# An adaLN hybrid backbone on one core: sums of squares taken inside the projections, residual additions followed block by block, and modulation rounds moved

## Chip, cores and metric

One core of a Trainium2 chip runs the whole program as one launch. The metric is the device time of an execution in microseconds (us). The kernel was timed three times before the change. One further execution was profiled; every row shown here comes from it.

## What is computed

Two layers run over 256 context tokens and 256 latent tokens, with D = 1024, all in float32. Only the latent tokens are returned.

```
x <- x + gate * RMSNorm_post(F(RMSNorm_pre(x) * (1 + scale) + shift))
m = SiLU(c) @ W_mod[layer] + b_mod[layer]      # (shift, scale, gate) for 2 sub-layers: 6 x 1024
layer 0: F = chunked gated linear attention, then dense SwiGLU (1024 -> 2816 -> 1024)
layer 1: F = RWKV-7 time mixing (latent output only), then top-2-of-8 SwiGLU experts (latent only)
rmsnorm(x, g) = x * rsqrt(mean(x*x) + 1e-6) * g
```

Context tokens have a modulation row of their own, from the same weights `W_mod`. In layer 1 the scan of the latent tokens starts from the final state of the scan of the context tokens.

## The kernel before

**Layout.** Activations lie transposed in SBUF: 128 partitions of features, 8 blocks of features (`KT = 8`), 512 tokens (`TOK`, columns 0 to 255 context, 256 to 511 latent). `X` is the residual stream. Everything is scheduled by hand: each engine has its own straight program, and waits on semaphores order them. A wait holds back everything behind it on its engine.

**A norm** (`norm_stats(n, width)`, once for ScalarE and once for TensorE) goes block by block. ScalarE squares block k into one of two buffers of `sq` and raises `sq_ready`. TensorE multiplies it by a matrix of ones and accumulates in PSUM bank 7, raising `sq_used`. After eight blocks ScalarE takes the root into `std`. VectorE then takes the reciprocal (L1367). For a norm ahead of a sub-layer VectorE multiplies `X` by it (`normalise`, L1374), and ScalarE applies the modulation (`modulate`, L1082, `h_ready` for each block). For a norm behind a sub-layer, `post` multiplies the output (L1381) and adds it to `X` with the gate (L1384), one `post_done` for each block, waiting for it before the next block. The norms are numbered: 0 ahead of attention, 1 behind its output projection `gla_o`, 2 ahead of the dense SwiGLU, 3 behind it, 4 and 5 ahead of the time mixing (context, latent), 6 behind its output projection `rw_o`, 7 ahead of the experts. All eight squares of a norm follow the end of what feeds it: for norms 2, 4, 5 and 7 the last residual addition, for 1, 3 and 6 the last copy out of PSUM.

**Modulation** comes in six rounds of 2048 columns (0 to 2 for layer 0, 3 to 5 for layer 1). A round reads 8 MB of `mod_w` as eight chunks of 1 MB. `mod_step(r, k, bank)` (L564) is TensorE's work on a chunk. VectorE copies the bank out (`mod_copy`, L1394), TensorE turns it (`mod_select`, L573, 8 matmuls), VectorE adds the bias (`add_bias`, L1400), then `pre_gains` and `post_gains` combine it with the norm's gains. Round 3 stands ahead of norm 2, round 4 between norm 2 and the dense SwiGLU, and round 5 between norm 3 and norm 4. Round 3 holds shift and scale of the time mixing (norms 4 and 5), round 4 its gate and the shift of the experts, round 5 scale and gate of the experts.

**Weights** stream through a ring of six 1 MB slots, all issued by SyncE in the order of the list `chunks`; the load of chunk n waits until chunk n-6 has been used. The ring is scratch memory during the RWKV scans, so the first chunk of `rw_k1` waits for the end of the context scan. GpSimd loads the small RWKV matrices (2.75 MB, `rw_small`) once for each segment, the second time after the context scan.

**Layer 1** runs `segment(0)` (norm 4, mixes, projections), the context scan, `segment(1)` (norm 5 and the same for latent tokens), the latent scan, the output projection `rw_o` and norms 6 and 7. In a segment VectorE prepares up to six mixes in two buffers `XJ` (`mix`, L1577). TensorE runs `hidden` on the first mix (L771), its second matrices (L782), then `hidden` on the second mix, and so on. The expert stage (L1011 to L1043) loops over eight experts, with rings of its own for its weights.

**The dense SwiGLU** has eleven pairs of up projections (L738, a block is 8 matmuls of 128x512) and a down projection (L748) that accumulates all eight output blocks over eleven chunks in the eight banks. Only when the last chunk is done does ScalarE copy out the eight banks (L1181, `O2`).

## Time and profile before

| | us |
|---|---|
| median of three runs | 2811.93 |
| lowest, highest | 2807.17, 2813.3 |
| the profiled execution | 2807.7 |
| its span, first to last instruction | 2805.9 |
| TensorE busy in it | 2576.8 |

The profiled execution takes 1.8 us more than its span. Times in rows count from the start of the span. A row of the timeline gives the start, the duration, the engine, the line of the kernel, the operation, what it writes and reads, how many instructions were merged, and in brackets the idle time ahead of it with what ended it. One float32 matmul of the kernel's code appears as two MATMUL records, so that the 64 matmuls of a projection of eight blocks are x128.

### The profile page before, as it was taken

To read this page: it belongs to the slowest core of one execution; us is meant where nothing else is said; L and a number is where in the kernel's file an instruction comes from. 1 tells how busy PE (TensorE), PEld (TensorE's weight loads), DVE (VectorE), ACT (ScalarE), POOL (GpSimd) and SP (SyncE) were. 2 spreads that over 40 slices of the span, in tenths; PEclk is the share of its full clock that TensorE was granted. 3 is DMA by queue.
4 is the path that set the end of the run, shared out by engine and by line. 5 is a ranking of instruction groups with operands and counts; after the bars stand their busy time and mean duration, and the time that the engine had idled before them with its cause. 6 is when DMAs were issued, how large, how long until landed. Compare 5 with 4: busy or idle time off the path is not lost.

```text
span 2805.9 us, 60500 instructions
## 1 busy us (share of the span) xinstructions
PE 2576.8 (92%) x27787; PEld 1788.2 (64%) x27788; DVE 664.7 (24%) x1098; ACT 468.3 (17%) x781; POOL 45.9 (2%) x146
## 2 busy tenths in 40 slices
PE   6998878999999878869888779999999999999998
PEld 2562732444444357868787578686969696959593
DVE  1033433100000176764876420000000010000001
ACT  3232012100000143443333120000000000000000
POOL 0000001200000000000000000000000000000000
PEclk9998979999999979989999789999999999999999
DMA  6215104622222320042002248888889897979794
GB/s 244 76 60 224 61 15 188 196 75 75 75 75 75 113 96 2 4 131 90 2 4 72 83 145 321 300 324 301 318 304 327 294 338 283 348 274 349 272 345 145
DMA packets 179201, 492.90 MB, mean 176 GB/s; under 512 B 9410, under 2 KB 73236, under 8 KB 172804
## 3 DMA queue, kind: packets, MB, share of 16 engines
q1 hardware_dynamic: 177156, 482.73, 48.3%
q0 software_dynamic: 1792, 6.19, 0.7%
q8 instruction: 232, 3.80, 0.5%
q14 instruction: 21, 0.17, 0.0%
HBM read 487.84 MB, written 1.05 MB: 174 GB/s over the span
## 4 chain that ended last, share of the span: by engine, by line
PE 53%; DVE 5%; ACT 1%; issue 1%; DMA 0%; POOL 0%; DVEq 0%; ACTq 0%; POOLq 0%
PE banks L1026 25%; PE banks L1043 14%; PE banks L809 6%; PE banks L606 3%; PE banks L1000 1%; PE banks L942 1%; PE banks L1011 1%; DVE ring_arena L1678 1%; PE banks L771 1%; DVE ring_arena L1683 1%; DVE rstd L1789 0%; DMA ring_arena<-in_rw_a 0%; PE banks L782 0%; DVE ring_arena L1690 0%; PE banks L543 0%
## 5 line engine op out<-in xcount | busy, mean ns | idle before, releaser
L1026 PEld LDWEIGHTS banks<-ring_arena 128*64 128x64 f32 x14336 | 687.1, 137 | 19.2 <-issue 18.4
L1026 PE MATMUL banks<-ring_arena 128*64 128x112 f32 x14336 | 694.2, 259 | 0.0
L1043 PE MATMUL banks<-ring_arena 128*112 128x512 f32 x896 | 385.8, 592 | 0.0
L606 PE MATMUL banks<-ring_arena 128*128 128x256 f32 (+1 forms) x1024 | 313.0, 467 | 24.4 <-ACT ring_arena L1082 12.7
L738 PE MATMUL banks<-ring_arena 128*128 128x512 f32 x704 | 305.3, 597 | 0.0
L1043 PEld LDWEIGHTS banks<-ring_arena 128*112 128x112 f32 x896 | 158.0, 177 | 221.9 <-issue 221.9
L606 PEld LDWEIGHTS banks<-ring_arena 128*128 128x128 f32 x1024 | 196.5, 193 | 140.3 <-issue 96.4
L1872 DVE TENSOR_TENSOR ring_arena<-ring_arena,banks 128x448 f32<-128x448 f32 x32 | 19.9, 621 | 1033.3 <-PE banks L1026 1033.3
L738 PEld LDWEIGHTS banks<-ring_arena 128*128 128x128 f32 x704 | 134.8, 192 | 169.8 <-issue 169.8
L809 PE MATMUL banks<-ring_arena 64*64 64x128 f32 (+1 forms) x6144 | 205.2, 260 | 31.2 <-DVE ring_arena L1683 13.1
L809 PEld LDWEIGHTS banks<-ring_arena 64*64 64x64 f32 x6144 | 192.8, 138 | 38.4 <-issue 22.7
L748 PE MATMUL banks<-ring_arena 128*128 128x512 f32 x352 | 151.3, 592 | 0.9 <-DVE ring_arena L1528 0.9
L748 PEld LDWEIGHTS banks<-ring_arena 128*128 128x128 f32 x352 | 66.8, 190 | 85.4 <-issue 83.7
L1367 DVE RECIPROCAL rstd<-std 128x512 f32<-128x512 f32 (+1 forms) x12 | 33.8, 2819 | 310.3 <-ACT std L1075 301.1
L1336 ACT ACTIVATE ring_arena<-banks 128x448 f32<-128x448 f32 x32 | 17.4, 544 | 512.7 <-PE banks L1026 512.7
L1242 ACT COPY ring_arena<-banks 128x1024 f32<-128x1024 f32 (+1 forms) x80 | 72.2, 928 | 111.4 <-DVE ring_arena L1678 98.3
L1108 ACT ACTIVATE ring_arena<-banks 128x256 f32<-128x256 f32 (+2 forms) x94 | 40.5, 439 | 284.7 <-PE banks L606 178.1
L1528 DVE TENSOR_TENSOR ring_arena<-ring_arena,banks 128x512 f32<-128x512 f32 x22 | 15.1, 687 | 290.2 <-PE banks L738 290.2
L564 PE MATMUL banks<-ring_arena 128*32 128x512 f32 x384 | 56.4, 700 | 20.0 <-DMA ring_arena<-in_mod_w 17.6
L543 PE MATMUL banks<-sq_ntmp,ones 128*128 128x256 f32 (+1 forms) x112 | 49.0, 588 | 26.3 <-ACT sq_ntmp L1073 25.5
L1326 ACT COPY ring_arena<-banks 112x512 f32<-112x512 f32 x18 | 9.6, 588 | 372.5 <-PE banks L1043 372.5
L1178 ACT ACTIVATE ring_arena<-banks 128x512 f32<-128x512 f32 x22 | 13.1, 597 | 278.6 <-PE banks L738 278.6
(293 smaller groups left out, 1827.8 us busy)
## 6 DMA issues: line engine op xcount, KB each, us to landing
ring_arena<-in_moe_w_gu SPq DMA_DIRECT2D x256, 896.0 KB, 5.5
ring_arena<-in_moe_w_d SPq DMA_DIRECT2D x112, 1024.0 KB, 7.1
ring_arena<-in_mod_w SPq DMA_DIRECT2D x48, 1024.0 KB, 7.3
ring_arena<-in_ff_w_gu SPq DMA_DIRECT2D x22, 1024.0 KB, 5.1
ring_arena<-in_rw_w_rkv SPq DMA_DIRECT2D x20, 1024.0 KB, 10.9
ring_arena<-in_gla_w_in SPq DMA_DIRECT2D x12, 1024.0 KB, 5.4
ring_arena<-in_ff_w_d SPq DMA_DIRECT2D x11, 1024.0 KB, 4.9
ring_arena<-in_gla_w_out SPq DMA_DIRECT2D x4, 1024.0 KB, 13.8
```

Of the source, the lines that this page charges most:

```text
L543: T.matmul(ps[7][:, 0:width], ones[:, :], sq[:, (k % 2) * TOK:(k % 2) * TOK + width], start=(k == 0), stop=(k == KT - 1)).then_inc(S["sq_u ...
L564: ins = T.matmul(bank[32 * j:32 * j + 32, :], csil[r // 3][:, k, :], w[:, j, :], start=(k == 0), stop=(k == KT - 1))
L606: ins = T.matmul(b[:, 0:width], w[:, k, j * P:j * P + P], src[:, k, :], start=(k == 0), stop=(k == KT - 1))
L738: ins = T.matmul(ps[4 * (p % 2) + 2 * ab + j][:, :], w[:, k, j * P:j * P + P], H2[:, k, :], start=(k == 0), stop=(k == KT - 1))
L748: ins = T.matmul(ps[j][:, :], w[:, k, j * P:j * P + P], HID[:, 2 * i + k, :], start=(i == 0 and k == 0), stop=(i == FT // 2 - 1 and k == 1))
L771: ins = T.matmul(b[0:cols, 0:SEG], w[:, k, :], src[:, k, :], start=(k == 0), stop=(k == KT - 1))
L809: ins = T.matmul(bank[rows[1 - r if cross and p >= HP // 2 else r], p, 0:x.shape[-1]], lhs[rows[r], p, :], x, start=first and p % (HP // 2 ...
L1026: ins = T.matmul(bank[CH * h:CH * h + CH, (c % 4) * CAP:(c % 4) * CAP + CAP], w[:, kk, c * P + CH * h:c * P + CH * h + CH], XG[:, 2 * kp + ...
L1043: ins = T.matmul(ps[6 + h][0:CAP, :], HX[:, 2 * u + k, :], w[:, k, 512 * h:512 * h + 512], start=(u == 0 and k == 0), stop=(u == WD_UNITS ...
L1108: C.activation(dst, src, func, **kw).then_inc(S["pj_out"], 1)
L1242: C.copy(w[d]["ZT"][:, :, half], scan_banks(d, 0)[:, :, half]).then_inc(za_s[d], 1)
L1367: link(Vv.reciprocal(rstd[:, 0:width], std[:, 0:width]))
```

## The change

The sum of squares of norms 1, 3 and 6 is taken inside the projection that feeds it: ScalarE squares each block right after it has copied it out, and TensorE takes the matmul with ones (`stat`) two blocks later, between the matmuls of the projection (for norm 3 in bank 0, within the last chunk of the down projection). The squares of norms 2, 4, 5 and 7 each wait for their own block's residual addition alone. Behind the dense SwiGLU, `post_half(0)` adds the context half to `X` first; the latent half follows within `segment(0)`, between the first and the second mix. Round 3 is wound into norm 2 and round 4 into norm 4 (`between_stats`); round 5 moves to the latent segment, between norm 5 and the first `hidden`. Their `mod_select`s stand in the second pair of up projections and ahead of the key projections. The first up projection waits for `h_ready` block by block. `O2` has another layout, and a third copy of SiLU(c) lies in `masks2`.

```diff
+        mod_rows = [ntmp[:, 512 * (r % 2):512 * (r % 2) + 512] if r < 3 else (at(22016, 512) if r == 3 else ntmp[:, 512:1024]) for r in range(6)]
 
...
         H2 = at(0, KT, TOK)
         HID = at(4096, FT, TOK)
         SIL = at(15360, 4, TOK)
...
         KK, KEY = at(0, SC, HP, CH), at(2048, SC, HP, CH)
         AA = [at(4096 + 2048 * d, SC, HP, CH) for d in range(2)]
@@ -223,7 +223,7 @@
...
         n_pairs = FT // 2
...
-        stream("ff_d", [A["ff_w_d"][0].rearrange("(k p) n -> p k n", p=P)[:, 2 * i:2 * i + 2, :] for i in range(11)], "ffd", 0, 1)
-        stream("mod5", mod_rounds(1, 2), "mod_mm", 40, 1)
+        ffd_views = [A["ff_w_d"][0].rearrange("(k p) n -> p k n", p=P)[:, 2 * i:2 * i + 2, :] for i in range(11)]
+        stream("ff_d", ffd_views[0:10], "ffd", 0, 1)
+        stream("ff_d_last", ffd_views[10:11], "ffo", 0, KT)
+        stream("mod4", mod_rounds(1, 1), "mod_mm", 32, 1)
...
         for sg in range(2):
+            if sg:
+                stream("mod5", mod_rounds(1, 2), "mod_mm", 40, 1)
             for n, name in ((1, "k"), (2, "v"), (0, "r"))[:2 + sg]:
                 stream(f"rw_{name}{sg}", cols256(rkv[n], 4), "pj", PJ1[sg] + 34 + 8 * "kvr".index(name), 2)
         stream("rw_o", cols256(A["rw_w_o"][0], 4), "pj", PROJ_END[1], 2)
...
-                for lat, name in enumerate(("rw_k1", "rw_o")):
+                for lat, name in enumerate(("mod5", "rw_o")):
                     if cid == first[name]:
...
-            pool.wait_ge(S["post_done"], 3 * KT)
+            pool.wait_ge(S["post_done"], 4 * KT)
...
+            def stat(n, k, width, bank=7):
+                pe.wait_ge(S["sq_ready"], KT * n + k + 1)
+                T.matmul(ps[bank][:, 0:width], ones[:, :], sq[:, (k % 2) * TOK:(k % 2) * TOK + width],
+                         start=(k == 0), stop=(k == KT - 1)).then_inc(S["sq_used"], 1)
...
-            project(first["gla_o"], Y1, TOK, 4)
-            norm_stats(1, TOK)
+            project(first["gla_o"], Y1, TOK, 4, lambda n: stat(1, n - 2, TOK) if n >= 2 else None)
+            stat(1, 6, TOK)
+            stat(1, 7, TOK)
...
+            def between_stats(n, width, r):
+
+                for k in range(4):
+                    mod_step(r, k, ps[6])
+                for k in range(KT):
+                    stat(n, k, width)
+                    if k < 4:
+                        mod_step(r, k + 4, ps[6])
             pe.wait_ge(S["csil"], 3)
-            for k in range(KT):
-                mod_step(3, k, ps[6])
-            norm_stats(2, TOK)
-            for k in range(KT):
-                mod_step(4, k, ps[5])
-            mod_select(3, ps[6])
-            mod_select(4, ps[5])
-
-
-            for k in range(KT):
-                pe.wait_ge(S["h_ready"], KT + k + 1)
+            between_stats(2, TOK, 3)
             for p in range(FT // 2):
                 for ab in range(2):
                     if ab == 0:
                         if p >= 2:
                             pe.wait_ge(S["ff_hid"], 2 * (p - 1))
                         if p == 1:
-                            pe.wait_ge(S["mod_add"], 5)
+                            mod_select(3, ps[6])
+                            pe.wait_ge(S["mod_add"], 4)
...
                         for k in range(KT):
+                            if p + ab + j == 0:
+                                pe.wait_ge(S["h_ready"], KT + k + 1)
...
-                ins.then_inc(S["ffd"], 1)
+                    if i == FT // 2 - 1:
+                        ins.then_inc(S["ffo"], 1)
+                        if j >= 2:
+                            stat(3, j - 2, TOK, 0)
+                if i < FT // 2 - 1:
+                    ins.then_inc(S["ffd"], 1)
+            stat(3, 6, TOK, 0)
+            stat(3, 7, TOK, 0)
             pe.wait_ge(S["ffd_out"], KT)
-            norm_stats(3, TOK)
-            for k in range(KT):
-                mod_step(5, k, ps[6])
-            mod_select(5, ps[6])
-            pe.wait_ge(S["mod_add"], 6)
...
             def segment(sg):
-                norm_stats(4 + sg, SEG)
+                if sg == 0:
+                    between_stats(4, SEG, 4)
+                else:
+                    norm_stats(5, SEG)
+                    for k in range(KT):
+                        mod_step(5, k, ps[6])
...
+                mod_select(4 + sg, ps[6])
                 project(first[f"rw_k{sg}"], mix(sg), SEG, 4)
+                pe.wait_ge(S["mod_add"], 5 + sg)
...
                     b = next_bank()
+                    if 2 * i + j >= 2:
+                        stat(6, 2 * i + j - 2, SEG)
                     for k in range(KT):
                         ins = T.matmul(by_chunk(b), w[:, k, j * P:j * P + P], YY[:, :, k, :],
                                        start=(k == 0), stop=(k == KT - 1))
                     ins.then_inc(S["pj"], 1)
-            T.transpose(ps[7][:, 0:P], ident[:, :], ident[:, :]).then_inc(S["gu_used"], GU_RING)
+            T.transpose(ps[6][:, 0:P], ident[:, :], ident[:, :]).then_inc(S["gu_used"], GU_RING)
+            stat(6, 6, SEG)
+            stat(6, 7, SEG)
             pe.wait_ge(S["pj_out"], tile[0])
-            norm_stats(6, SEG)
             norm_stats(7, SEG)
...
-            act.wait_ge(S["pj_out"], tile[0])
-            norm_stats(1, O1, TOK)
-            act.wait_ge(S["post_done"], KT)
-            norm_stats(2, X, TOK)
+                act.wait_ge(S["pj_out"], tile[0])
+                square(1, k, O1[:, k, :], TOK)
+            root(1, TOK)
+            norm_stats(2, X, TOK, 0)
...
-            act.wait_ge(S["ffd"], FT // 2)
             for k in range(KT):
-                C.copy(O2[:, k, :], ps[k][:, :]).then_inc(S["ffd_out"], 1)
-            act.wait_ge(S["ffd_out"], KT)
-            norm_stats(3, O2, TOK)
+                v = O2[:, :, SEG * k:SEG * k + SEG]
+                act.wait_ge(S["ffo"], k + 1)
+                C.copy(v, ps[k][:, :].rearrange("p (s c) -> p s c", s=2)).then_inc(S["ffd_out"], 1)
+                act.wait_ge(S["ffd_out"], k + 1)
+                square(3, k, v, TOK)
+            root(3, TOK, 0)
...
-                act.wait_ge(S["post_done"], 2 * KT)
-                norm_stats(4 + sg, X[:, :, tok_cols(sg)], SEG)
+                norm_stats(4 + sg, X[:, :, tok_cols(sg)], SEG, KT + KT * sg)
...
-            act.wait_ge(S["pj_out"], tile[0])
-            norm_stats(6, O3, SEG)
-            act.wait_ge(S["post_done"], 3 * KT)
-            norm_stats(7, X[:, :, tok_cols(1)], SEG)
+                act.wait_ge(S["pj_out"], tile[0])
+                square(6, k, O3[:, k, :], SEG)
+            root(6, SEG)
+            norm_stats(7, X[:, :, tok_cols(1)], SEG, 3 * KT)
...
+            def post_half(sg):
+
+                rs = rstd[:, tok_cols(sg)]
+                link(Vv.reciprocal(rs, std[:, tok_cols(sg)]))
+                for k in range(KT):
+                    v, cols = O2[:, sg, SEG * k:SEG * k + SEG], tok_cols(sg)
+                    link(Vv.tensor_tensor(v, v, rs, ALU.mult))
+                    Vv.scalar_tensor_tensor(X[:, k, cols], v, post_gain(0, 1, k, sg), X[:, k, cols],
+                                            ALU.mult, ALU.add).then_inc(S["post_done"], 1)
+                n_post[0] += KT
+                dve.wait_ge(S["post_done"], n_post[0])
...
             post(1, O1, TOK, 0, 0, (0, 1))
+            normalise(2, 1, X, TOK)
             mod_copy(3, ps[6])
-            normalise(2, 1, X, TOK)
-            mod_copy(4, ps[5])
             add_bias(3, ps[6])
-            add_bias(4, ps[5])
             link(pre_gains(1, 0))
-            link(post_gains(1, 0))
+            dve.wait_ge(S["csil"], 3)
+            Vv.tensor_copy(csil[2], csil[1]).then_inc(S["csil"], 1)
...
-            post(3, O2, TOK, 0, 1, (0, 1))
-            mod_copy(5, ps[6])
-            add_bias(5, ps[6])
-            link(pre_gains(1, 1))
-            link(post_gains(1, 1))
+            dve.wait_ge(S["std_ready"], 4)
+            post_half(0)
...
                     ins.then_inc(S["mix_ready"], 1)
+                    if j == 1 and sg == 0:
+                        post_half(1)
+                        mod_copy(4, ps[6])
+                    if j == 4 and sg == 1:
+                        mod_copy(5, ps[6])
                     if j == 2:
                         sums(sg)
                     if j == 3:
+                        add_bias(4 + sg, ps[6])
+                        if sg == 0:
+                            link(post_gains(1, 0))
+                        else:
+                            link(pre_gains(1, 1))
+                            link(post_gains(1, 1))
                         if sg == 0:
```

## Rows read from the trace of the kernel before

**Rows 1.** The page: the chain that ended last, shares of the span by line.

```profile
PE banks L1026 25%; PE banks L1043 14%; PE banks L809 6%; PE banks L606 3%; PE banks L1000 1%; PE banks L942 1%; PE banks L1011 1%; DVE ring_arena L1678 1%; PE banks L771 1%; DVE ring_arena L1683 1%; DVE rstd L1789 0%; DMA ring_arena<-in_rw_a 0%; PE banks L782 0%; DVE ring_arena L1690 0%; PE banks L543 0%
```

**Rows 2.** Stretches: length, busy and count by engine, granted clock, DMA share, GB/s.

```profile
510.00:804.00 294.00, 293.24 (x684) 129.54 (x682) 15.07 (x22) 12.54 (x21) 1.32 (x3) 1.00 0.26 85
...
1647.00:2806.00 1159.00, 1146.24 (x15576) 889.28 (x15576) 70.08 (x142) 72.22 (x130) 0.00 (x0) 0.99 0.84 301
```

**Rows 3.** Timeline from the end of `gla_o` to the first up projection.

```profile
447.42 0.60 ACT L1108 ACTIVATE ring_arena<-banks 128x512 f32<-128x512 f32 x1 [6.27 <-PE banks L606]
...
454.45 0.63 ACT L1073 ACTIVATE sq_ntmp<-ring_arena 128x512 f32<-128x512 f32 x1 [0.23 <-PE banks L543]
...
456.29 0.60 ACT L1075 ACTIVATE std<-banks 128x512 f32<-128x512 f32 x1 [1.22 <-PE banks L543]
...
473.45 1.15 ACT L1073 ACTIVATE sq_ntmp<-x_stream 128x512 f32<-128x512 f32 x2 [16.56 <-DVE x_stream L1384]
...
484.44 0.60 ACT L1075 ACTIVATE std<-banks 128x512 f32<-128x512 f32 x1 [1.22 <-PE banks L543]
...
489.19 7.97 ACT L1082 ACTIVATE ring_arena<-sq_ntmp,mods,gain 128x256 f32<-128x256 f32 x16 [4.15 <-DVE sq_ntmp L1374]
...
493.90 1.06 PE L573 MATMUL banks<-ident,ring_arena 128*128 128x8 f32 x8
...
497.90 4.61 PE L738 MATMUL banks<-ring_arena 128*128 128x512 f32 x5
```

**Rows 4.** Timeline from the end of the down projection into `segment(0)`.

```profile
955.46 4.01 ACT L1181 COPY ring_arena<-banks 128x512 f32<-128x512 f32 x8 [165.26 <-PE banks L748]
...
969.96 0.60 ACT L1075 ACTIVATE std<-banks 128x512 f32<-128x512 f32 x1
...
975.86 1.07 PE L564 MATMUL banks<-ring_arena 128*32 128x512 f32 x8 [0.75 <-DMA ring_arena<-in_mod_w]
...
990.00 6.72 PE L543 MATMUL banks<-sq_ntmp,ones 128*128 128x256 f32 x16 [0.28 <-DVE mods L1400]
...
996.76 0.38 ACT L1075 ACTIVATE std<-banks 128x256 f32<-128x256 f32 x1 [0.79 <-PE banks L543]
...
997.25 1.75 DVE L1367 RECIPROCAL rstd<-std 128x256 f32<-128x256 f32 x1 [6.88 <-ACT std L1075]
...
1006.82 6.42 DVE L1577 SCALAR_TENSOR_TENSOR ring_arena<-ring_arena,vecs 128x256 f32<-128x256 f32 x16
...
1010.18 6.50 PE L771 MATMUL banks<-ring_arena 128*128 128x256 f32 x16 [13.45 <-issue]
...
1023.50 3.72 PE L771 MATMUL banks<-ring_arena 128*128 128x256 f32 x16
```

**Rows 5.** Timeline of the start of `segment(1)`: SyncE's loads, the statistics, the first `hidden`.

```profile
1227.77 71.14 SPq L395 DMA_DIRECT2D ring_arena<-in_rw_w_rkv  x10
...
1228.23 4.75 PE L543 MATMUL banks<-sq_ntmp,ones 128*128 128x256 f32 x16 [2.01 <-ACT sq_ntmp L1073]
...
1247.79 5.46 PE L771 MATMUL banks<-ring_arena 128*128 128x256 f32 x16 [14.82 <-issue]
```

**Rows 6.** The chain at the same place: the last small matrix that lands.

```profile
1233.23 12.89 DMA ring_arena<-in_rw_a
```

**Rows 7.** GB/s of all transfers in 40 slices of 1 us, 1226 to 1266.

```profile
GB/s 16 0 22 242 357 365 368 360 257 243 245 235 231 288 360 358 387 401 387 350 346 351 347 348 346 348 349 349 347 350 112 10 0 0 0 16 0 0 0 0
```

**Rows 8.** The same in slices of 1.25 us, 446 to 496 (rounds 3 and 4).

```profile
GB/s 0 39 197 419 184 0 0 0 0 85 216 419 302 374 347 413 419 419 433 426 433 413 419 446 433 426 282 33 0 0 0 0 118 347 400 419 406 363 362 349
```

**Rows 9.** Timeline from the end of `rw_o` to norm 7.

```profile
1597.18 0.38 ACT L1108 ACTIVATE ring_arena<-banks 128x256 f32<-128x256 f32 x1 [3.07 <-PE banks L942]
...
1602.91 0.38 ACT L1075 ACTIVATE std<-banks 128x256 f32<-128x256 f32 x1 [0.79 <-PE banks L543]
...
1612.43 0.48 DVE L1384 SCALAR_TENSOR_TENSOR x_stream<-ring_arena,gain,x_stream 128x256 f32<-128x256 f32 x1
...
1619.43 0.38 ACT L1075 ACTIVATE std<-banks 128x256 f32<-128x256 f32 x1 [0.79 <-PE banks L543]
```

41 lines of the change are left out of this document (24 added, 17 removed).

## The prediction, made before the changed kernel had run

> **What bounds the kernel now.** I read the page first. TensorE is busy for 2576.8 of 2805.9 us, and the chain that ended last runs mostly through its matmuls, the experts' L1026 and L1043 ahead [rows 1]. The table of stretches splits that share: in the up projections TensorE is busy for 293.24 of 294 us at full clock, among the experts for 1146.24 of 1159 us [rows 2]. The change touches neither loop, so it can only act in the gaps between stages. Those I read in the timeline: from `gla_o` to the first up projection (447.4 to 497.9) [rows 3], from the down projection to the first `hidden` (955.5 to 1010.2) [rows 4], the start of `segment(1)` (1227.8 to 1247.8) [rows 5] and the end of `rw_o` (1597.2 to 1619.4) [rows 9]. In each the reader is to see one serial chain: copy, squares and sums, root, reciprocal, additions, then all of that again. The modulation's chunks lie beside it. The transfer rates [rows 7, 8] I read last, for the loads that move.
>
> **Unit costs.** A matmul of 128x512 is two records of 293.24/684 = 0.43 us [rows 2], so 0.86 us; one of 128x256 takes 3.72/8 = 0.46 us, say 0.43 without the ramp [rows 4]. All of this is at the granted clock 1.00, 2.4 GHz. At 1.2 GHz it doubles: the first five records after the gap take 4.61 us [rows 3].
>
> **Norms 1 and 2.** Six of the eight sums now stand between matmuls of `gla_o` ahead of its end: 6 x 0.86 = 5.1 us more there, so the last copy starts at 447.4 + 5.1 = 452.6. Its square starts 0.63 us later, and the root starts 456.29 - 454.45 = 1.84 us after the last square starts [rows 3]: 455.05 instead of 456.29, 1.2 us saved. Most of what leaves the serial chain comes back in the projection, because TensorE was already the slower partner in that loop. The additions then end at 473.45 - 1.2 = 472.2. Of norm 2 only the last square is left behind them: root at 472.2 + 1.84 = 474.0, or 474.9 if the last sum runs at 1.2 GHz; I take 474.4 instead of 484.44, 10.0 us saved. Round 3 fills TensorE's time under the additions (four steps ahead of the sums, four between the first four), 0.9 to 1.1 us a step [rows 4] against additions (473.45 - 456.29 - 0.60 - 3.4 for root and reciprocal)/8 = 1.65 us apart; its chunks come from a ring that is emptied as before. Round 4 leaves this place, where reciprocal and modulation had covered it, so nothing is gained by that.
>
> The up projection no longer waits for all eight modulated blocks. The first is ready 489.19 - 484.44 + 7.97/8 = 5.75 us after the root starts [rows 3], at 480.2, against a first matmul at 497.90: 17.7 us. The blocks come 1.0 us apart. Starting at 1.2 GHz, TensorE uses up the ramp (4.6 us) while it would wait anyway, and finishes the first output block at 480.2 + 4.3 + 5.5 x 0.86 = 489.2; before it was 497.9 + 4.3 + 11 x 0.43 = 506.9, again 17.7. If the ramp doesn't come during the staggered start, the block takes 8 x 1.72 and ends at 494: 13.0 at the low end. The high end is 18.1, with the root at 474.0. Into the second pair come `mod_select(3)` and a wait for VectorE: 1.06 us [rows 3] and 0.28 us for the answer [rows 4]. Behind that wait only matmuls of this pair queue; VectorE's products start later, but TensorE asks for them a pair later. **Net 17.7 - 1.3 = 16.4 us (11.7 to 16.8).**
>
> **Norms 3 and 4.** Within the last chunk a block takes 2 x 0.86 and, from the third on, 0.86 more for a sum; ScalarE needs 0.50 + 0.63 and a short wait for a block, less than TensorE's 2.57. Five sums lie ahead of the last block's end, so the last copy starts at 955.46 + 5 x 0.86 = 959.8, where before the first one did [rows 4]. Copy, square and the loading of the root's table (1.28 us) end at about 962.3, sum 8 likewise; the root starts at 962.4, not 969.96: 7.5 us. It ends at 963.0. A half reciprocal takes 1.75 us [rows 4], then eight context additions. One takes (1612.9 - 1605.1)/8 = 0.98 us with its product in norm 6, where root and reciprocal end at 1605.1 [rows 9]; without the wait between blocks I take 0.90, so they end at 972.0. The square of the last block follows, and the root of norm 4 starts 1.84 - 0.21 - 0.43 = 1.2 us after it (square and sum at half the width), at 973.3. Where the page of norms said 996.76, this leaves out the latent additions, the round 5 turn and eight serial sums.
>
> TensorE may be later than that. The sixth to eighth chunk of round 4 wait for slots: the sixth for the last chunk of the down projection (959.5), the seventh and eighth for the first two steps (963 and 964). Loads landed some 5 us after such a release: the seventh step of round 5 started at 975.86 on the arrival of its chunk, and the first, which frees the slot, stands right behind the sums whose root starts at 969.96, so it ended near 970.8 [rows 4]. So they arrive near 964.5, 968.3 and 970.8, and the last step ends at 971.7 to 972.6. Four sums of 0.43 (0.86 at 1.2 GHz) and two squares that wait for buffers follow: root at 973.9 to 976.5. I take 974.8: 22.0 us saved (19.8 to 23.5). All that follows to the first `hidden` keeps its distance. VectorE now has the latent half between the first and the second mix: 1.8 + 7.2 + 0.7 (`mod_copy`) + 3.3 us. On the old time axis the first mix is ready at 1006.8 + 3.2 = 1010.0, the second then at 1023.0, and TensorE asks for it at 1023.50 [rows 4]. That cover is 0.5 us; without it each further us of VectorE costs one. The third mix and the running sums come 2 us later, and the key projection of 28 us hides them. `mod_select(4)` costs 1.1 us. **Net 20.9 us (18.0 to 22.4).**
>
> **Norm 5 and round 5, the loss.** After the context scan SyncE issues six chunks of `rw_k1` and `rw_v1` at 1227.77 [rows 5], which nobody needs for 40 us, while GpSimd's small matrices land at 1246.1 and gate the first `hidden` with the first mix (1247.79) [rows 5, 6]. After the change TensorE stands between norm 5 and `hidden` until all eight chunks of round 5 have been used: 8.39 MB plus the 2.75 MB of small matrices. Before, 6.29 + 2.75 MB took from 1229 to 1256.5, 350 GB/s when only large chunks moved, about 240 when both did [rows 7]. That is 18.0 us for the chunks and 9.5 for the small ones. Modulation chunks run at about 420 GB/s [rows 8]: 8.39/0.42 = 20.0, plus 9.5, ends at 1258.8. With 0.6 us for the release and a last step of 1.9 us at 1.2 GHz, `hidden` starts at 1261.3: 13.5 us late. The seventh and eighth chunk need slots that the first steps free by about 1240, so they don't break the stream. The queue behind the waiting step is all of TensorE's segment, which is its bound from here to the scan, so the delay counts in full. The key weights of this segment come behind round 5 and are in by 1275, 10 us ahead of their use. `mod_select(5)` adds 1.1. The ends: round 5 at 420 GB/s with the small loads behind it, 3.5 us; everything at the mixed 240 GB/s, 11.1/0.24 = 46 us, 30 us. I take the sum by parts, as it reproduces the old window. **Net -14.6 us (-31 to -4.6).**
>
> The Trainium skill (DMA: Bandwidth & Descriptors, Where 436 GB/s comes from) says that about 358 GB/s of HBM bandwidth binds a load into SBUF. The 413 to 446 GB/s of this trace [rows 8] speak against it for these chunks. By the page the large part would take 23.4 us and the loss would be 3.4 us larger.
>
> **Norms 6 and 7.** Six sums of 0.43 us go into `rw_o`: the last copy starts at 1599.8, its square 0.4 later, the root 1.2 after that at 1601.4 and not 1602.91, 1.5 us. The additions (ending at 1612.9 [rows 9]) end at 1611.4, the root of norm 7 starts at 1612.7 to 1613.1, not 1619.43. What follows hangs on it. The weights of the first expert start with the end of `rw_o`, 1.3 to 2.6 us later than before against that end, but had 30 us of cover. **Net 6.5 us (6.0 to 6.8).** The other edits (the layout of `O2`, the third copy of SiLU(c), GpSimd's count for the router) cost VectorE or ScalarE at most 0.3 us where TensorE works.
>
> **The sum.** 16.4 + 20.9 - 14.6 + 6.5 = 29.2 us. The profiled execution took 2807.7, which gives 2778.5. It lies 4.2 us under the median of the runs; from the median the sum gives 2782.7. I take 2781.
>
> **Rivals.**
> - *The loads of `segment(1)` share badly*, at 240 GB/s to the end: 30 us of delay. For it: the rate stays low for six slices while both queues move [rows 7]. Against: it recovers to 350. Gain 29.2 - 16.5 = 12.7, time 2797.
> - *Round 5 is nearly hidden*, because the small matrices give way and land last: 3.5 us of delay. For it: they already land late, at 1246.1 [rows 6]. Gain 39, time 2771.
> - *The change doesn't do what it says*: the sums inside projections wait for ScalarE, so that norms keep their serial length and only the block-wise start is left, which the loss in `segment(1)` eats. ScalarE's 1.2 us against TensorE's 2.6 to 4.3 us a block speaks against it. About 2809.
> - *Slower: a lower clock in the dense stages.* With fewer idle stretches between them TensorE could be granted less in the up projections and among the experts. They last 294 and 1159 us at 1.00 and 0.99 [rows 2]. A mean fall by 2% costs the whole 29.2 us; from there on the kernel is slower, at 3% it takes 2826. Against: 294 us without a pause held 1.00.
>
> **How the numbers follow.** Forecast 0.77 (2773 to 2790, the ends of the first, second and fourth part and 4 us either way for the third), bad sharing 0.10, hidden 0.05, not what it says 0.04, clock 0.04. For 8 in 10 the range goes from the hidden case to just short of bad sharing: 2771 to 2795. A measurement of this kernel tells about 0.2% from no change, 5.6 us: faster 0.92, same 0.04, slower 0.04.
>
> **What would show it.** Right: the first L738 some 28 us after the end of `gla_o` instead of 51; `hidden` of `segment(0)` 28 to 31 us after the down projection's last block instead of 55; L564 steps between 1233 and 1261 on the old axis that each wait for `in_mod_w`, and the first L771 of `segment(1)` 33 us after the context scan instead of 20; the first expert 9 us nearer to the new end of `rw_o`. Wrong: an L543 inside a projection that waits for ScalarE, a wait ahead of the second L771 for VectorE, or a granted clock under 0.98 in the dense stages.

## The result, and the profile after

| | before | after |
|---|---|---|
| median of the runs, us | 2812.61 (4 runs) | 2782.91 (4 runs) |
| lowest, highest | 2807.17, 2815.33 | 2779.43, 2784.71 |
| the profiled execution, its span | 2807.7, 2805.9 | 2782.67, 2780.9 |

The ratio is 0.9897 with a 95% interval of 0.9881 to 0.9913: faster by 29.7 us at the medians, forecast 31 (2781); the difference is clear of noise, and small, 1% of the time. The two spans differ by only 25.0 us, since the changed kernel's profiled execution reached `gla_o` 5.55 us later, ahead of anything that the change touches (395.35 against 389.80; a second profiled execution of the same kernel had 386.49). So all that follows is read from marker to marker and not on the common time axis. The marker for the end of the context scan is SyncE's first load behind it, at 1227.77 before and 1195.98 after. "Root n" is the start of ScalarE's root of norm n:

| from ... to (first instruction of each) | before | after | gained | forecast |
|---|---|---|---|---|
| `gla_o` to root 1 | 66.49 | 65.23 | 1.3 | 1.2 |
| root 1 to root 2 | 28.15 | 20.07 | 8.1 | 8.8 |
| root 2 to first up projection | 13.46 | 6.05 | 7.4 | 7.7 |
| up to first down projection | 306.19 | 307.34 | -1.2 | -1.3 |
| down projection to root 3 | 165.87 | 158.53 | 7.3 | 7.5 |
| root 3 to root 4 | 26.80 | 13.60 | 13.2 | 14.5 |
| root 4 to `hidden` of `segment(0)` | 13.42 | 13.42 | 0 | 0 |
| that `hidden` to the end of the context scan | 217.59 | 216.39 | 1.2 | -1.1 |
| scan's end to `hidden` of `segment(1)` | 20.02 | 34.94 | -14.9 | -13.5 |
| that `hidden` to root 6 | 355.12 | 352.20 | 2.9 | 0.4 |
| root 6 to root 7 | 16.52 | 11.24 | 5.3 | 5.0 |
| root 7 to the end of the span | 1186.47 | 1186.54 | -0.1 | 0 |
| sum | | | 30.5 | 29.2 |

The timeline of the changed kernel from `gla_o`'s last copy to the first up projection, answering [rows 3]:

```profile
458.11 0.60 ACT L1142 ACTIVATE ring_arena<-banks 128x512 f32<-128x512 f32 x1 [6.46 <-PE banks L614]
458.74 0.63 ACT L1097 ACTIVATE sq_ntmp<-ring_arena 128x512 f32<-128x512 f32 x1
...
460.58 0.60 ACT L1101 ACTIVATE std<-banks 128x512 f32<-128x512 f32 x1 [1.22 <-PE banks L544]
...
469.47 2.08 PE L544 MATMUL banks<-sq_ntmp,ones 128*128 128x512 f32 x2
...
477.94 0.63 ACT L1097 ACTIVATE sq_ntmp<-x_stream 128x512 f32<-128x512 f32 x1 [1.42 <-PE banks L544]
478.80 0.63 ACT L1097 ACTIVATE sq_ntmp<-x_stream 128x512 f32<-128x512 f32 x1 [0.23 <-PE banks L544]
...
480.65 0.60 ACT L1101 ACTIVATE std<-banks 128x512 f32<-128x512 f32 x1 [1.22 <-PE banks L544]
...
486.70 3.75 PE L749 MATMUL banks<-ring_arena 128*128 128x512 f32 x4 [6.08 <-ACT ring_arena L1116]
```

The last copy comes 10.7 us later than in [rows 3], only half of it the late start: the other half is the sums in the projection. Root follows last copy after 2.47 us instead of 8.9. The additions end at 477.70. Behind them two squares stand ahead of root 2 and not one as forecast, both of them waiting for TensorE's sums, which free the two buffers. The up projection starts 6.05 us after that root, 28.6 after the last copy, instead of 50.5. The sum at 469.47 took 2.08 us, twice its usual time: the granted clock was 0.50, which is 1.2 GHz, from 468.4 to 471.8, and this is what put the sums behind.

The timeline from the end of the down projection into `segment(0)`, answering [rows 4]:

```profile
949.50 2.93 PE L544 MATMUL banks<-sq_ntmp,ones 128*128 128x512 f32 x6
...
949.71 0.58 ACT L1216 COPY ring_arena<-banks 128x512 f32<-128x512 f32 x1 [1.03 <-PE banks L759]
...
951.27 1.28 ACT L1101 ACT_TABLE_LOAD   x1
...
952.57 0.60 ACT L1101 ACTIVATE std<-banks 128x512 f32<-128x512 f32 x1
...
962.74 1.06 PE L570 MATMUL banks<-ring_arena,masks 128*32 128x512 f32 x8 [0.74 <-DMA ring_arena<-in_mod_w]
963.74 2.40 PE L544 MATMUL banks<-sq_ntmp,ones 128*128 128x256 f32 x8
...
966.17 0.38 ACT L1101 ACTIVATE std<-banks 128x256 f32<-128x256 f32 x1 [0.79 <-PE banks L544]
...
979.59 5.78 PE L784 MATMUL banks<-ring_arena 128*128 128x256 f32 x16 [13.45 <-issue]
...
988.76 4.43 DVE L1620 SCALAR_TENSOR_TENSOR ring_arena<-ring_arena,vecs 128x256 f32<-128x256 f32 x11
992.19 1.13 PE L784 MATMUL banks<-ring_arena 128*128 128x256 f32 x4
```

The last copy is followed by its square, by the table for the root, and by the root 2.86 us after the copy began. The context additions end at 961.92, and root 4 comes 4.25 us later: round 4's last step waited 0.74 us for its chunk, and the last four sums (2.40 us) stand behind it. So TensorE's queue set root 4 and not VectorE; the load's share of it is the 0.74 us. The latent half held VectorE until 988.76, and the second `hidden` at 992.19 has no wait in brackets: the cover of half a microsecond sufficed.

The timeline of the start of `segment(1)`, answering [rows 5]; the steps between the second and the last are like these, each with a wait for `in_mod_w`:

```profile
1201.31 1.06 PE L570 MATMUL banks<-ring_arena,masks 128*32 128x512 f32 x8
1205.29 1.59 PE L570 MATMUL banks<-ring_arena,masks 128*32 128x512 f32 x8 [2.92 <-DMA ring_arena<-in_mod_w]
1211.22 1.93 PE L570 MATMUL banks<-ring_arena,masks 128*32 128x512 f32 x8 [4.35 <-DMA ring_arena<-in_mod_w]
...
1229.06 1.93 PE L570 MATMUL banks<-ring_arena,masks 128*32 128x512 f32 x8 [0.61 <-DMA ring_arena<-in_mod_w]
1230.92 4.73 PE L784 MATMUL banks<-ring_arena 128*128 128x256 f32 x16
```

The same stretch's transfer rates in 40 slices of 1 us, 1196 to 1236, and two of its load groups (the last number is the median time from issue to landing), answering [rows 6, 7]:

```profile
GB/s 25 156 377 377 410 426 336 336 332 303 352 336 315 324 340 352 382 398 393 399 414 423 401 426 397 430 414 422 434 418 369 360 347 345 352 349 346 347 350 348
...
ring_arena<-in_mod_w SPq DMA_DIRECT2D x8, 1024.0 KB, 19.6
...
ring_arena<-in_rw_a POOLq DMA_DIRECT2D x1, 512.0 KB, 24.4
```

Six steps run at 1.2 GHz (1.93 us against 1.06) between waits of 0.6 to 4.4 us. The last small matrix needed 24.4 us; in [rows 6] it needed 12.9. It landed at 1225.8, 5 us ahead of `hidden`, so here it held nothing. But without the round's steps `hidden` would have waited for it until then, and that second wait was not in the forecast.

Norms 6 and 7 in the timeline, answering [rows 9]:

```profile
1581.50 0.38 ACT L1142 ACTIVATE ring_arena<-banks 128x256 f32<-128x256 f32 x1 [3.05 <-PE banks L964]
...
1583.12 0.38 ACT L1101 ACTIVATE std<-banks 128x256 f32<-128x256 f32 x1 [0.79 <-PE banks L544]
...
1594.36 0.38 ACT L1101 ACTIVATE std<-banks 128x256 f32<-128x256 f32 x1 [0.79 <-PE banks L544]
```

And the dense stages as two stretches (columns as in [rows 2]):

```profile
490.00:794.00 304.00, 302.91 (x709) 134.22 (x707) 17.83 (x29) 17.86 (x30) 20.61 (x71) 1.00 0.25 82
1622.00:2781.00 1159.00, 1146.25 (x15576) 889.25 (x15576) 69.92 (x141) 72.22 (x130) 0.00 (x0) 0.99 0.83 301
```

The clock is 1.00 and 0.99 as before, with 1146.25 us of TensorE in the same 1159: the rival of a lower clock is out.

### The profile page after: what moved, and what is told of

It is laid out like the page before. It is cut to its first block, busy times and chain, and to the rows that moved or that the text cites. A ratio compares the mean times of both kernels' runs of the same rounds, so it can differ in the third digit from the quotient of the medians.

```text
span 2780.9 us, 60560 instructions
## 1 busy us (share of the span) xinstructions
PE 2575.1 (93%) x27787; PEld 1784.0 (64%) x27788; DVE 664.4 (24%) x1108; ACT 470.0 (17%) x781; POOL 45.5 (2%) x146
## 4 chain that ended last, share of the span: by engine, by line
PE 53%; DVE 5%; ACT 1%; DMA 1%; issue 1%; DVEq 0%; SPq 0%; ACTq 0%
PE banks L1049 25%; PE banks L1066 14%; PE banks L829 6%; PE banks L614 3%; PE banks L1023 1%; DMA ring_arena<-in_mod_w 1%; PE banks L964 1%; PE banks L1034 1%; DVE ring_arena L1732 1%; PE banks L784 1%; DVE ring_arena L1737 1%; DVE rstd L1843 0%; PE banks L800 0%; ACT ring_arena L1277 0%; DVE ring_arena L1744 0%
## 5 line engine op out<-in xcount | busy, mean ns | idle before, releaser
L1402 DVE RECIPROCAL rstd<-std 128x512 f32<-128x512 f32 (+1 forms) x11 | 30.5, 2770 | 126.3 <-ACT std L1101 117.2
L656 PE MATMUL banks<-ring_arena 128*128 128x256 f32 x256 | 55.5, 379 | 0.0
```

Source lines behind the costliest of these rows:

```text
L656: ins = T.matmul(b[:, 0:256], H[:, k, t * P:t * P + P], w[:, k, :], start=(k == 0), stop=(k == KT - 1))
L1402: link(Vv.reciprocal(rstd[:, 0:width], std[:, 0:width]))
```

## Experiments

All edits are made to the changed kernel. "Local" is a distance between two markers of the table above in the profiled execution; the changed kernel's value stands behind "against". Ratios are to the kernel before.

### What round 5's place costs

**round5_early**: round 5 behind norm 4, ahead of the first `hidden` of `segment(0)`, its chunks issued behind round 4's.

```diff
         stream("mod4", mod_rounds(1, 1), "mod_mm", 32, 1)
+        stream("mod5", mod_rounds(1, 2), "mod_mm", 40, 1)
...
                     between_stats(4, SEG, 4)
+                    pe.wait_ge(S["std_ready"], 5)
+                    for k in range(KT):
+                        mod_step(5, k, ps[7])
                 else:
                     norm_stats(5, SEG)
-                    for k in range(KT):
-                        mod_step(5, k, ps[6])
...
```

> Round 5 of the modulation stands behind the sums of norm 4 (bank 7, once norm 4's root has read it) and no longer in the latent segment; all else as in the changed kernel. Theory (the loss in the latent segment is the wait for eight chunks that only start to load when the context scan ends): the first hidden of the latent segment starts about 20 us after the scan's end, as before the change, and not 35 us; the context segment pays instead only what the loads of round 5 exceed the reciprocal, modulation and first mix, the last step ending near 32 us after norm 3's root and hidden about 5 us later than now. Net 10 us faster than the changed kernel, about 2773. Rival (the cost is TensorE's own time for eight steps and the turn): moving it changes nothing, 2783. Second rival (the bigger queue of loads in the context segment makes the key weights late): hidden is right but the key projection of the context segment waits for loads, 2780 or more.

Measured: median 2779.87 (4 runs, 2775.55 to 2783.26), ratio 0.9891 (0.9868 to 0.9915), which doesn't tell it from the changed kernel; the 2773 expected was missed by 7. Locally the expectation held: scan's end to `hidden` 20.21 against 34.94, root 4 to `hidden` of `segment(0)` 18.45 against 13.42. That is 14.7 less 5.0 us. From `gla_o` to the first expert's first matmul it is 9.9 us shorter (1216.96 against 1226.85). Part of what blurs the total is a tail of 5 us that this profiled execution has at its end, in code that the edit doesn't touch, shown in the last section; whether the other three had it isn't known. So the move of round 5 cost what its loads cost, and the local lengths show it better than the medians do.

**quarter_round5**: round 5 where the change has it, but each chunk a quarter (a kernel that leaves out three quarters of round 5's weights).

```diff
-                stream("mod5", mod_rounds(1, 2), "mod_mm", 40, 1)
+                stream("mod5", [v[:, :, 0:512] for v in mod_rounds(1, 2)], "mod_mm", 40, 1)
```

> Each of the eight chunks of round 5 loads only 512 of its 2048 columns (256 KB and not 1 MB); the steps multiply what lies in the rest of the slot, so the scale and gate of the experts are not computed rightly. TensorE's and VectorE's work is unchanged. Theory (bytes behind the scan's end set the delay: 20 us for round 5 and 9.5 for the small matrices): with 2.1 MB the steps are done by 16 us after the scan's end, ahead of the first mix, and the first hidden starts 20 us after it and not 35: about 2768. Rival (the latency from issue to landing, slot by slot): the seventh and eighth chunk still land 5 us after slots come free, hidden 25 us or more after the scan's end, 2773 or more.

Measured: 2769.58 (2 runs), ratio 0.9851 (0.9824 to 0.9877). Scan's end to `hidden` is 20.21. TensorE still takes all eight steps. Its timeline:

```profile
1197.57 2.78 PE L570 MATMUL banks<-ring_arena,masks 128*32 128x512 f32 x24
...
1209.13 1.94 PE L570 MATMUL banks<-ring_arena,masks 128*32 128x512 f32 x8 [0.89 <-DMA ring_arena<-in_mod_w]
1212.46 2.90 PE L784 MATMUL banks<-ring_arena 128*128 128x256 f32 x6 [1.40 <-DMA ring_arena<-in_rw_a]
```

The last wait is again for `in_rw_a`, as before the change. The loss lies in the loads and not in the matmuls. The edit makes the rows of a chunk shorter too (2 KB instead of 8), so it doesn't tell their bytes from their packets.

**round5_late**: the loads of round 5 unmoved, but TensorE takes the steps behind the second `hidden`, so that the first need not wait for them.

```diff
-                    for k in range(KT):
-                        mod_step(5, k, ps[6])
...
+                    for k in range(KT):
+                        mod_step(5, k, ps[6])
+                    project(first[f"rw_k{sg}"], mix(sg), SEG, 4, lambda n: mod_select(5, ps[6]) if n == 4 else None)
```

> In the latent segment round 5 stands behind both hidden stages and their second matrices, ahead of the key projection, instead of ahead of the first hidden. Its turn stands in the key projection. Theory (the loads are what takes 33 us; TensorE's own steps take 8 us at full clock): hidden starts 20 us after the scan's end, and the key projection 51 us after it instead of 58: 6 to 7 us faster than the changed kernel, 2776. Rival (the cost is the same wherever TensorE takes the steps): 2783.

Measured: 2794.09 (3 runs), ratio 0.9936 (0.9909 to 0.9962), 11 us behind the changed kernel, where 6 to 7 ahead of it were expected; 4.4 of the 11 are the router's clock in its profiled execution (see both_moves). Scan's end to `hidden` is 27.18, neither 20 nor 35, scan's end to the key projection 62.06 against 57.95, and to the third `hidden` of the segment 154.1 against 146.3. Its timeline:

```profile
1221.83 5.23 PE L784 MATMUL banks<-ring_arena 128*128 128x256 f32 x16 [21.79 <-DMA ring_arena<-in_rw_a]
...
1244.42 5.36 PE L570 MATMUL banks<-ring_arena,masks 128*32 128x512 f32 x48
...
1251.09 1.06 PE L570 MATMUL banks<-ring_arena,masks 128*32 128x512 f32 x8 [1.30 <-DMA ring_arena<-in_mod_w]
```

Three things were missing from my expectation. The ring has six slots: chunks seven and eight are issued only when the first steps have run, from 1245.55 on, so the round ends with waits after all. The key weights come behind them: the first, issued at 1247.27, landed at 1256.62, TensorE waited 1.98 us for it, and the first half of the key projection, part of it at 1.2 GHz, took 16.9 us against 13.9. And the small matrices are themselves late. Here are the two queues (packets, MB, share; q1 is SyncE's, q0 GpSimd's) and the last small matrix from issue to landing, first in round5_late, then in round5_early:

```profile
q1 hardware_dynamic: 864, 6.29, 44.9%
q0 software_dynamic: 784, 2.75, 18.2%
...
ring_arena<-in_rw_a POOLq DMA_DIRECT2D x1, 512.0 KB, 21.7
```

```profile
q1 hardware_dynamic: 6240, 6.29, 50.4%
q0 software_dynamic: 784, 2.75, 22.3%
...
ring_arena<-in_rw_a POOLq DMA_DIRECT2D x1, 512.0 KB, 12.6
```

Both kernels have 6.29 MB in SyncE's queue beside the same 2.75 MB. With the key and value weights that is 6240 packets of 1 KB, with round 5's chunks 864 of 7.3 KB on average. Against small packets GpSimd's 3.5 KB ones get through in 12.6 us, against large ones in 21.7. The reason shows in the counts of a stretch in which both queues have work, 1202 to 1212 of the changed kernel, then 1234 to 1242 of the kernel before:

```profile
q1 hardware_dynamic: 312, 2.29, 72.7%
q0 software_dynamic: 306, 1.02, 28.6%
```

```profile
q0 software_dynamic: 491, 1.70, 76.0%
q1 hardware_dynamic: 513, 0.52, 29.5%
```

The queues move equal numbers of packets, 306 to 312 and 491 to 513, whatever the size. (round5_late has 322 to 318 in 1202 to 1212, round5_early 513 to 507 in 1206 to 1214.) So with SyncE's packets at 7.3 KB GpSimd's queue gets a third of the bytes, 102 GB/s, and with 1 KB three quarters, 212 GB/s. The Trainium skill (DMA: Bandwidth & Descriptors, Queues, rings and completion order) says that a DMA engine takes the queues in turn, a packet at a time. These counts agree with turns of equal length; how many packets of the profile make up a turn they don't show.

### What the sums in the projections are worth

**serial_sums**: norms 1, 3 and 6 again with all squares and sums behind their projection, the rest of the change kept.

```diff
-            project(first["gla_o"], Y1, TOK, 4, lambda n: stat(1, n - 2, TOK) if n >= 2 else None)
-            stat(1, 6, TOK)
-            stat(1, 7, TOK)
+            project(first["gla_o"], Y1, TOK, 4)
+            norm_stats(1, TOK)
...
```

> For norms 1, 3 and 6 all squares and all sums stand behind the projection again; the copies out of the down projection still follow block by block. All else as in the changed kernel. Theory (a sum inside a projection pushes back the last block by its own length, so only the loop's waits are saved): root of norm 1 1.3 us later, of norm 3 about 3 us, of norm 6 1.6 us: 6 us slower than the changed kernel, 2789. Rival (taking sums out of the serial chain saves their whole length, 7 us for a norm of 512 columns): 14 us or more, 2797.

Measured: 2788.46 (4 runs, 2782.86 to 2794.13), ratio 0.9926 (0.9899 to 0.9953), an interval that overlaps the changed kernel's; its span of 2781.1 is the changed kernel's 2780.9, with a start to `gla_o` 3.1 us shorter. Locally `gla_o` to root 1 is 66.49 against 65.23, the down projection to root 3 160.39 against 158.53, and `hidden` of `segment(1)` to root 6 352.56 against 352.20: 3.5 us in all, where 6 were expected. Norm 3 costs 1.9 and not 3: without the sums the last copy comes 4.3 us sooner after the first down projection, and root 3 follows it after 9.0 us instead of 2.9. Norm 6 shows 0.4 and not 1.6: from the last copy to root 6 it is 5.7 us again, against 1.6, but the first 8.9 us of `rw_o` had a granted clock of 0.82 here and 0.68 in the changed kernel. So the first edit in the title carries about a tenth of the gain, at most a sixth if norm 6 is put at its 1.6.

**one_sum**: VectorE adds up the squares beside the projection and TensorE takes one sum per norm (1, 3 and 6) instead of eight.

```diff
+            def stat_once(m, width, bank=7):
+                pe.wait_ge(S["acc"], m)
+                T.matmul(ps[bank][:, 0:width], ones[:, :], ntmp[:, 0:width], start=True, stop=True).then_inc(S["sq_used"], 1)
...
-            project(first["gla_o"], Y1, TOK, 4, lambda n: stat(1, n - 2, TOK) if n >= 2 else None)
-            stat(1, 6, TOK)
-            stat(1, 7, TOK)
+            project(first["gla_o"], Y1, TOK, 4)
+            stat_once(1, TOK)
...
```

> For norms 1, 3 and 6 VectorE adds up the squares of the eight blocks in SBUF while the projection runs, and TensorE takes a single matmul with ones behind it, instead of eight, six of them inside the projection. Theory (inside a projection each sum costs TensorE its full 0.86 or 0.43 us and pushes the last block back): the last copy comes 5.1, 4.3 and 2.6 us earlier, an addition of 0.7 (0.4) us comes on top behind the last square, so the roots come 4.4, 3.7 and 2.0 us earlier: 10 us faster than the changed kernel, about 2773. Rival (the sums fill slots that TensorE would idle through anyway, so they cost nothing): the extra addition makes each root 0.5 to 0.8 us later, 2785.

Measured: 2773.38 (4 runs, 2766.59 to 2778.91), ratio 0.9867 (0.9838 to 0.9897). The median is the one expected, but its interval overlaps the changed kernel's; the router ran at the lower clock in its profiled execution (see both_moves), which cost some 4 us there. `gla_o` to root 1 is 60.90 against 65.23, the down projection to root 3 154.63 against 158.53, and the first matmul of `rw_o` to root 6 32.55 against 34.92: 4.3, 3.9 and 2.4 us, expected 4.4, 3.7 and 2.0. The last addition, the one sum and root 1:

```profile
445.34 0.69 DVE L1430 TENSOR_TENSOR sq_ntmp<-sq_ntmp 128x512 f32<-128x512 f32 x1 [6.17 <-ACT sq_ntmp L1095]
446.09 1.12 PE L555 MATMUL banks<-sq_ntmp,ones 128*128 128x512 f32 x2 [2.14 <-DVE sq_ntmp L1430]
447.25 0.60 ACT L1099 ACTIVATE std<-banks 128x512 f32<-128x512 f32 x1 [2.01 <-PE banks L555]
```

The addition costs 0.7 us of an engine that had 6.17 us free between two of them; the sums taken out of TensorE's queue are worth 4.3.

### What following by block is worth

**squares_after**: the squares of norms 2, 4, 5 and 7 wait for all eight additions, and the rounds' steps stand ahead of them.

```diff
-                for k in range(4):
+                for k in range(KT):
                     mod_step(r, k, ps[6])
                 for k in range(KT):
                     stat(n, k, width)
-                    if k < 4:
-                        mod_step(r, k + 4, ps[6])
...
-                        act.wait_ge(S["post_done"], posts + k + 1)
+                        act.wait_ge(S["post_done"], posts + KT)
```

> The squares of norms 2, 4, 5 and 7 wait for all eight residual additions again, and rounds 3 and 4 stand ahead of the sums instead of between them. Theory (the squares and sums hide behind the additions): norm 2's root comes 8 us later, norm 4's about 3 (its sums follow the last step of round 4, which waits for loads), norm 7's 5: 16 us slower than the changed kernel, 2799. Rival (the additions, on VectorE, are slowed by sharing or the sums are bound by round 3 and 4 anyway): under 8 us, 2790.

Measured: 2799.2 (5 runs), ratio 0.9951 (0.9935 to 0.9967): 16 us behind the changed kernel. Root 1 to root 2 is 27.37 against 20.07, root 3 to root 4 15.01 against 13.60, root 6 to root 7 17.05 against 11.24; together 14.5, expected 8, 3 and 5. Its profiled execution is 20.3 us longer from `gla_o` to the end; of the rest 3.8 are the router, which ran at the lower clock here (told under both_moves). In its timeline all of norm 2 stands behind one wait of 16.56 us:

```profile
474.51 1.15 ACT L1095 ACTIVATE sq_ntmp<-x_stream 128x512 f32<-128x512 f32 x2 [16.56 <-DVE x_stream L1417]
```

Norm 4 gives up only 1.4. Its eight steps, without sums among them and with waits of 1.31 and 1.53 us for chunks, end 10.1 us after root 3 instead of 11.2, and then eight sums follow (4.9 us) instead of four (2.4).

**all_blocks**: the first up projection waits for all eight modulated blocks again.

```diff
+            for k in range(KT):
+                pe.wait_ge(S["h_ready"], KT + k + 1)
...
-                            if p + ab + j == 0:
-                                pe.wait_ge(S["h_ready"], KT + k + 1)
```

> The first up projection waits for all eight modulated blocks again, all else as in the changed kernel. Theory (the staggered start runs through the slow clock while TensorE would wait): the first output blocks are 6 us later, the 64 records of the first pair end 36.7 us after the first block is ready instead of 30.5; about 2789. Rival (what is gained at the start is lost to the ramp of the clock, which only comes with unbroken work): under 2 us, 2784.

Measured: 2789.91 (5 runs), ratio 0.9933 (0.9912 to 0.9953). Root 2 to the first down projection is 319.41 against 313.39, so the staggered start is worth 6.0 us, as expected.

**both_halves**: `post_half(1)` directly behind `post_half(0)` instead of between the mixes.

```diff
             dve.wait_ge(S["std_ready"], 4)
             post_half(0)
+            post_half(1)
...
                     if j == 1 and sg == 0:
-                        post_half(1)
                         mod_copy(4, ps[6])
```

> The latent half of the additions behind norm 3 comes right after the context half on VectorE, ahead of norm 4's reciprocal, and not between the first and second mix. Theory (norm 4's root waits for round 4 and its sums, 4.7 us after the context half is done, so VectorE has that much free time there): the reciprocal of norm 4 starts 8.6 - 4.7 = 3.9 us later, 2787. Rival (all of the half's 8.6 us counts): 2791.5. Second rival (the half between the mixes already delays the second hidden, and moving it gives that back): 2783.

Measured: 2782.06 (2 runs), ratio 0.9893 (0.9839 to 0.9946), too wide to tell. Root 3 to `hidden` of `segment(0)` is 31.08 against 27.02, and this row and the next show why it is 4.1 and not the 9 us that the latent half takes:

```profile
964.74 0.39 ACT L1101 ACTIVATE std<-banks 128x256 f32<-128x256 f32 x1 [0.79 <-PE banks L544]
...
970.09 1.75 DVE L1402 RECIPROCAL rstd<-std 128x256 f32<-128x256 f32 x1
```

Half of the latent additions lie under the wait for round 4 and root 4; only what reaches past the root delays the reciprocal, which starts 5.35 us after root 4 instead of 0.49. Root 4 itself comes 12.80 us after root 3, against 13.60: here round 4's last step did not wait for its chunk.

### Both improvements together

**both_moves** is one_sum and round5_early in one kernel; **changed_again** is the changed kernel without an edit, on the same chip.

> The changed kernel with two edits together: one addition in PSUM for the sums in place of the partial ones in the projections (as in the run with one sum), and round 5 of the modulation back ahead of the scan's end (as in the run with round 5 early). The theory that each cost lies in a stretch of its own has the local gains add: gla_o's start to root 1 61 us in place of 65.2, the first down projection to root 3 154.6 in place of 158.5, the scan's end to the context segment's hidden projection 20 in place of 34.9, root 4 to the latent segment's hidden projection 18.5 in place of 13.4. That is 4.3 + 3.9 + 14.7 - 5.0 = 17.9 us locally, of which one sum pays back some 5 at norm 6 and the first key projection, so about 12 to 14 us less than the changed kernel: a median near 2770. The rival, that round 5's loads hold up the key projection's weights once the stretch before them is shorter, has the gain stay at one edit's: 2774 to 2780.

> The changed kernel once more, with no edit, on the same chip as the run before it, so that the two are told apart: both theories have 2782 to 2783 again, and the stretch from the last expert's start to the end of the span at either 155.6 or 161 us.

Measured: both_moves 2767.86 (5 runs, 2756.57 to 2773.53), ratio 0.984 (0.9817 to 0.9862); changed_again 2778.85 (4 runs, 2773.64 to 2783.32), ratio 0.9886 (0.987 to 0.9901). The intervals don't meet: both_moves beats both kernels, by 44 and 11 us. Expected were 2770, and 2782 to 2783 for the changed kernel, which came out 4 us lower; its end was the short one. (The expectation names the two segments the wrong way round: the latent `hidden` follows the scan.) The local lengths of both_moves are the sum of the two edits': `gla_o` to root 1 60.88, the down projection to root 3 154.63, root 4 to `hidden` 18.41, scan's end to `hidden` 20.22. From `gla_o` to the end of the span it takes 2370.9 us, changed_again 2385.3.

One part of this expectation rested on a misreading. The payback of 5 us at the first key projection wasn't there: in one_sum I had taken a row at 989.78 for the start of a projection that began at 985.38, 11.46 us after the second `hidden`, exactly as in the changed kernel. What did take back 4.5 us in both_moves is the router: root 7 to the first expert is 32.3 us against changed_again's 27.8. Its matmuls of eight columns are one row of the timeline, first of changed_again, then of both_moves:

```profile
1596.33 3.77 PE L985 MATMUL banks<-ring_arena 128*128 128x8 f32 x32
```

```profile
1582.15 6.83 PE L985 MATMUL banks<-ring_arena 128*128 128x8 f32 x32
```

The same code, 3.77 us at a granted clock of 0.94 and 6.83 at 0.50, which is 1.2 GHz. Of the twelve profiled executions eight have 3.7 to 4.0 us there, and four have 6.83: one_sum, both_moves, squares_after and round5_late.

## Why the prediction was right, and where it was off

**Norms 1 and 2.** Forecast 17.7 to the first up projection, measured 16.75. Root 1 came as worked out (1.26 for 1.2). Root 2 gave 8.1 for 8.8, because one sum and the step ahead of it ran at 1.2 GHz and a second square came to stand behind the additions; all_blocks and one_sum, where no sum slowed, had one square there and 19.0 instead of 20.07 from root to root. The turn cost 1.15 for 1.3.

**Norms 3 and 4.** Root 3 gave 7.3 for 7.5. Root 4 gave 20.5 for 22.0, inside its stated 19.8 to 23.5; the term that was too favourable is the last step of round 4. The forecast had its chunk there 8.4 us after root 3 and TensorE waiting for it. Measured is a start at 10.2, and only 0.74 of that is the wait: in both_halves, where the chunk was in time, TensorE reached the step at 9.4, since sums stand between its steps, 1.63 us for a sum and a step. That the additions don't set root 4 was right; that the loads set it was so for the last 0.8 us alone.

**Norm 5 and round 5.** The term of 13.5 was 14.9, and its working was right only in total. I had added 9.5 us for the small matrices to 20.0 for the chunks, taking 240 GB/s as the price of a mixture and 350 as that of large chunks alone. That misread [rows 7]: there both queues moved until 1245.6, at 231 to 257 for five slices and then at 288 to 401 for six. With round 5 in the queue both moved until 1225.4, at 303 to 352 up to 1212 and at 382 to 434 from there on, so hardly a slice had the chunks alone. The last chunk was there 33.1 us after the scan's end, where the sum by parts had 31.0. What the sum left out is the other consumer: the small matrices landed at 1201.44 + 24.4 = 1225.8, 29.9 us after the scan's end. Had TensorE not waited for the round at all, it would by this row have saved 5 us and not 15; round5_late, whose last two chunks came later, saved 7.8 there (and lost it again behind). So between a third and a half of the loss is the wait for the round's last steps, and the rest comes with its transfers alone. That the queues take turns by packets is shown by their equal counts; no run had round 5's full volume in smaller packets, so what smaller ones would give back is not measured.

The Trainium skill's limit of about 358 GB/s (DMA: Bandwidth & Descriptors, Where 436 GB/s comes from) didn't bind here either: thirteen slices in a row lie between 393 and 434 GB/s.

**Norms 6 and 7.** Root 6 to root 7 gave 5.3 for 5.0. Of `hidden` to root 6, 2.9 for 0.4, `rw_o` to root 6 gave 1.6 for 1.5. Some 1.4 us are shorter scan work that the change doesn't touch: from the third `hidden` to `rw_o` the kernel before took 207.4 us, the changed one 205.95 and 206.3 in two executions, and the edited ones 205.2 to 208.7. The rest is the term of -1.1 for the turn: the stretch between the first and third `hidden` grew by 0.2 only. Where 1.2 was measured for -1.1, 1.4 lie between the key projection and the scan's end, which took 193.7 us before, 192.3 in both executions of the changed kernel and 192.1 to 195.5 in the edited ones. No run shows a cause for either difference.

**What the total hid.** That 29.2 came out as 30.5 owes something to luck: the rows without a scan missed by 3.5 us together, root 4 and round 5 above all, and the two rows with scans gave 4.8 back.

## What to carry to other kernels

Work moved off a serial chain into a loop that TensorE bounds comes back as that loop's time: sums inside three projections were worth 3.5 us, while giving the additions to an idle VectorE was worth 8.2 more at norms 1 and 3. When a load is moved, price what it does to every other consumer of the same transfer engines: here two queues moved equal numbers of packets, so the sizes of their packets decided who waited, and the loser was a set of small matrices on another queue. And a ring of slots ties a load to the consumption of an earlier one, so that postponing TensorE's steps postpones the loads that were to be hidden.

## What the runs showed of the hardware

Identical code differs in three places by a few microseconds (the scans come on top, see above), so a median of four runs hardly tells 5 us. The start to `gla_o` took 386.35 to 395.35 us; the router ran at either clock (above); and the end of the span has two lengths. The last VectorE instruction ended 2.5 us ahead of the span's end in ten profiled executions, 7.7 us in round5_early and 8.2 in all_blocks. The output's 576 packets are the same; what differs in the closing stretch is the queue that brings instructions, first in round5_early, then in the changed kernel:

```profile
q1 hardware_dynamic: 576, 1.05, 13.5%
q8 instruction: 5, 0.08, 2.0%
```

```profile
q1 hardware_dynamic: 576, 1.05, 17.2%
q8 instruction: 2, 0.03, 0.7%
```

Three more pieces of code are fetched in the last 12 us, two of them behind the last VectorE instruction (1.0 and 4.3 us after it). What decides that no run here settles; it is why round5_early's profile (2773.8) lies 5 us nearer to the changed kernel's than its local lengths do.
